# A two-block transformer layer on one core: front sums, last queries and weight pieces dealt anew to the steps of the first attention

## The chip, the cores and the metric

The kernel runs on one NeuronCore of a Trainium2 chip, in one launch. The metric is device time in microseconds. The kernel before takes 1286.5 us, the median of three runs (1285.71, 1286.50, 1286.87).

A core has five engines, each with its own program in order, which meet by semaphores. TensorE (PE) multiplies and transposes into eight PSUM banks, VectorE (DVE) and ScalarE (ACT) do elementwise work, GpSimd (POOL) does elementwise work beside them, and SyncE (SP) issues loads.

## The reference

Two transformer blocks run in turn over 512 tokens of width 1024, in float32. The change touches the first block's attention alone:

```python
h = rmsnorm(x, attn_pre_g); proj = h @ w_in
# sliding window: 8 heads, 2 key heads, window 128, with sinks
o_swa = swa_attention(q_s, k_s, v_s, sinks, slopes[:8])
# 8 more heads, three branches each, every one a softmax of its own
s_c = q . k_cmp   # 31 compressed keys
s_s = q . k_slc   # selected blocks: at 512 tokens, all of them
s_w = q . k_win   # window of 512
o_nsa = g0 * (p_c @ v_cmp) + g1 * (p_s @ v_slc) + g2 * (p_w @ v_win)
mix = concat([o_nsa, o_swa]) @ w_o
x = x + rmsnorm(mix, attn_post_g)
```

Then follow a gated MLP with a depthwise convolution, an embedding gate, and a second block (neighbourhood attention, retention, MLP, final norm).

## The kernel before, in words

**Precision.** Each float32 operand is split into a high and a low part, and a dense product is three matmuls: high weight by high input, high by low, low by high (lines 593, 594 and 595 in `triple`). The input's parts are AH and AL; BH and BL later hold attention's outputs.

**Weights.** A *piece* is 128x512 weights, loaded by SyncE into one of five raw buffers. ScalarE makes its high part (`hi`, L1323), VectorE or, in the attention, GpSimd its low part (`lo`, L2943). TensorE then runs 12 matmuls of 512 columns on it (`part`). Conversion runs four pieces ahead. Pieces go in the order of the list that `plan` builds, and in the attention that order comes from the table `FILL1`: for every step, the pieces that TensorE runs in it.

**Units and steps.** The first attention has 28 units. Units 0 to 7 are sliding-window ("swa"). Then come four rounds of five: one *compressed* unit (units 8, 13, 18, 23) and four wide ones ("sl" and "wn", for two key groups g). A software pipeline runs over steps s:

- TensorE in step s: the pieces of `FILL1[s]`; the transposes of unit s-2 (L813; of a compressed unit L854); the scores of unit s+1 (L799 and L800; compressed L843); the value products of unit s-3 (L826 and L827, the compressed part L866).
- VectorE in step s: the scaling of finished queries or keys (L2095, L2097), the softmax bias and minimum of unit s (L2191; compressed L2233 to L2241), sums of outputs (`out_add` L2214, `out_low` L2219), the low parts of the transposed probabilities of unit s-3 (`rest`, L2207), the reciprocal for unit s-1 (L2272), and last the low parts of new queries (`stacked`, L2109) or keys (`doubled`, L2104 and L2105).
- ScalarE in step s: first what the pieces of step s-1 finished (`filled`: queries L1411, keys L1406 and L1407, or a front sum), the exponentials of unit s (L1510), weights' high parts, the copies of the transposed probabilities of unit s-2 (`turned`, L1516), then `out_part` (L1521), which waits for the values of unit s-3, and `out_high` (L1525).
- GpSimd in step s: the normalising of unit s-1 (L2969), which the transposes of step s+1 need, then low parts of weights.

A piece of "w_swa" or "w_nsa" is half a projection: two make one query pair q(J), J from 0 to 7 (or a key pair). A piece of "w_o_swa" is a whole *front sum*: the sliding-window heads' share of one of the eight blocks of the output projection. ScalarE copies it out of its bank (L1533, `filled`) to ACC1, and the end of attention adds the rest to it.

**Buffers.** The eight banks are handed out in the order in which they are given back, when the program is built. Who takes a bank waits for its last reader. Queries live in four buffers QS, so q(J) waits until the scores that read q(J-2) are done. Low and high keys of the sliding window are in KS1["s"]. The first three ACC1 buffers lie over KS1["s"], the other five over AH, the high input.

## Time and profile before

| | |
|---|---|
| median of the runs | 1286.5 us |
| profiled execution | 1286.42 us, of which the span is 1284.5 us |
| TensorE busy | 1263.0 us, 98% of the span |
| VectorE, ScalarE, GpSimd busy | 786.6, 647.9, 216.9 us |
| chain that ended last | 90% TensorE |
| mean granted clock of TensorE | 0.996 |

The span is the time from the first to the last instruction of the profiled execution. A row of the timeline shows start, duration, engine, line, operands by the program's names and a count; in brackets, the idle time before it and who ended it. Consecutive matmuls overlap at their ends, so what one costs is read from start to start. The whole time is a little over a millisecond; steps 7 to 27 of the first attention run from 100 to 218 us.

### The profile page before, as it was taken

How to read it: one execution, taken by the hardware profiler on the slowest of the kernel's cores; microseconds unless marked ns; L12 is line 12 of the kernel's file. 1: busy time of each engine (PE TensorE's matmuls, PEld its weight loads, DVE VectorE, ACT ScalarE, POOL GpSimd, SP SyncE). 2: the span in 40 equal slices, each digit the busy share in tenths (PEclk: the TensorE clock that was granted, in tenths of full speed). 3: DMA queues.
4: the chain of work that ended last, by engine and by line, in shares of the span. 5: the costliest groups of instructions: out<-in, count | busy, mean ns of one | idle time of the engine just before them, and what ended most of it. 6: DMA issues, size and time to landing. Idle time of an engine off the chain costs nothing.

```text
span 1284.5 us, 16448 instructions
## 1 busy us (share of the span) xinstructions
PE 1263.0 (98%) x6004; PEld 1045.6 (81%) x6004; DVE 786.6 (61%) x1465; ACT 647.9 (50%) x1261; POOL 216.9 (17%) x234
## 2 busy tenths in 40 slices
PE   9999999999999999999999999999999999999998
PEld 8887888878888888888787777887888888888887
DVE  6689687686645565356788876589644343343334
ACT  6787788554335433233555655586533252332344
POOL 0064555000100011001002101032311030110111
PEclk9998999999999999999999999999999999999999
...
GB/s 275 86 50 34 42 41 26 170 82 99 90 100 98 98 90 99 99 96 68 115 91 98 76 56 68 131 112 68 98 99 92 97 75 118 79 115 89 100 90 67
DMA packets 64626, 118.20 MB, mean 92 GB/s; under 512 B 7713, under 2 KB 12193, under 8 KB 64289
## 3 DMA queue, kind: packets, MB, share of 16 engines
...
## 4 chain that ended last, share of the span: by engine, by line
PE 90%; DVE 4%; ACT 2%; issue 2%; DMA 1%; POOL 1%; POOLq 0%; SPq 0%; DVEq 0%; ACTq 0%
PE bank L593 26%; PE bank L595 25%; PE bank L594 25%; PE bank L813 2%; PE bank L693 2%; PE bank L694 2%; PE bank L695 2%; PE bank L826 1%; PE bank L827 1%; PE bank L799 1%; PE bank L800 1%; PE bank L767 1%; DVE q2p L2191 0%; DMA praw<-in_pT 0%; DVE r_bc L2086 0%
## 5 line engine op out<-in xcount | busy, mean ns | idle before, releaser
L2022 DVE TENSOR_TENSOR wl<-raw,wh 128x512 fp32r<-128x512 f32 (+2 forms) x360 | 267.5, 754 | 325.5 <-ACT wh L1323 324.8
L1323 ACT ACTIVATE wh<-raw 128x512 fp32r<-128x512 f32 (+1 forms) x398 | 242.2, 618 | 284.7 <-PE bank L595 273.7
L593 PE MATMUL bank<-AH,wh 128*128 128x512 f32 (+1 forms) x848 | 333.8, 394 | 2.1 <-DVE AL L2036 0.8
L595 PE MATMUL bank<-AH,wl 128*128 128x512 f32 (+1 forms) x848 | 329.3, 388 | 0.0
L594 PE MATMUL bank<-AL,wh 128*128 128x512 f32 (+1 forms) x848 | 327.0, 386 | 0.0
L593 PE MATMUL bank<-BH,wh 128*128 128x512 f32 x624 | 247.7, 397 | 1.6 <-ACT acc L1533 1.6
L595 PE MATMUL bank<-BH,wl 128*128 128x512 f32 x624 | 244.6, 392 | 0.0
L594 PE MATMUL bank<-BL,wh 128*128 128x512 f32 x624 | 243.0, 389 | 0.0
L595 PEld LDWEIGHTS bank<-AH,wl 128*128 128x128 f32 x848 | 159.6, 188 | 35.8
L593 PEld LDWEIGHTS bank<-AH,wh 128*128 128x128 f32 x848 | 159.9, 189 | 35.2 <-issue 2.9
L594 PEld LDWEIGHTS bank<-AL,wh 128*128 128x128 f32 x848 | 159.7, 188 | 33.0 <-issue 0.2
L593 PEld LDWEIGHTS bank<-BH,wh 128*128 128x128 f32 x624 | 117.3, 188 | 27.7 <-ACT acc L1533 2.1
L595 PEld LDWEIGHTS bank<-BH,wl 128*128 128x128 f32 x624 | 117.2, 188 | 27.2
L594 PEld LDWEIGHTS bank<-BL,wh 128*128 128x128 f32 x624 | 117.2, 188 | 25.6 <-issue 0.5
L2985 POOL TENSOR_TENSOR BL<-tmp,BH 128x512 fp32r<-128x512 f32 x22 | 28.6, 1300 | 354.4 <-ACT BH L1632 354.4
L3013 POOL TENSOR_TENSOR AL<-tmp,AH 128x512 fp32r<-128x512 f32 x32 | 40.6, 1303 | 269.6 <-ACT AH L1954 269.6
L2943 POOL TENSOR_TENSOR wl<-raw,wh 128x512 fp32r<-128x512 f32 x38 | 50.2, 1323 | 100.2 <-ACT wh L1323 100.2
L1510 ACT ACTIVATE pp<-pp,small 128x128 f32<-128x128 f32 (+2 forms) x96 | 50.2, 525 | 7.5 <-DVE small L2191 7.1
L2969 POOL TENSOR_SCALAR pp<-pp,small,gates 128x128 f32<-128x128 f32 (+1 forms) x64 | 40.9, 654 | 34.2 <-DVE small L2272 34.2
L2805 DVE TENSOR_TENSOR X<-X,bank 128x512 f32<-128x512 f32 x46 | 31.5, 686 | 24.3 <-PE bank L595 24.2
L2869 DVE SCALAR_TENSOR_TENSOR tmp<-bank,r_bc 128x512 f32<-128x512 f32 x32 | 22.0, 691 | 27.6 <-PE bank L595 16.1
L2191 DVE CUSTOM_DVE_ANT_0 pp<-bank,dn 128x512 f32<-128x512 f32 (+1 forms) x64 | 27.5, 486 | 15.9 <-PE bank L800 15.7
...
## 6 DMA issues: line engine op xcount, KB each, us to landing
raw<-in_w_dn SPq DMA_DIRECT2D x104, 256.0 KB, 2.7
...
```

The costliest lines, as they stand in the source:

```text
L593: t.matmul(o, w, xh, start=start, stop=False, skip_group_check=skip)
L594: t.matmul(o, w, xl, start=False, stop=False, skip_group_check=skip)
L595: return t.matmul(o, wl, xh, start=False, stop=stop, skip_group_check=skip)
L1323: a.activation(W[i % NW].h[:, 0:n], RAW[i % NRAW][:, 0:n], ACT.Copy).then_inc(*s_wh.up(i))
L1510: m = a.activation(o, o, ACT.Exp, bias=m4[:, qb:qb + 1], scale=-1.0, accum_out=s4[:, qb:qb + 1])
L2022: v.tensor_tensor(w.l[:, 0:n], RAW[i % NRAW][:, 0:n], w.h[:, 0:n], ALU.subtract).then_inc(*s_wl.up(i))
L2191: m = v.tensor_tensor_reduce(o, b[:, col:col + w], bias(qb), scale, init, ALU.add, ALU.min, m4[:, qb:qb + 1])
L2805: v.tensor_tensor(chunk(X, c), chunk(X, c), bank.ap(key)[:, :], ALU.add).then_inc(*s_sv.up(done))
L2943: g.tensor_tensor(w.l[:, 0:n], RAW[i % NRAW][:, 0:n], w.h[:, 0:n], ALU.subtract).then_inc(*s_wlg.up(i))
L2969: g.tensor_scalar(o, o, r, by, ALU.mult, ALU.mult).then_inc(*s_nmg.up((u, qb)))
L2985: g.tensor_tensor(x.l, tmp.ap(("u", k))[:, 0:T], x.h, ALU.subtract).then_inc(*s_xlg.up(("ff", k)))
L3013: g.tensor_tensor(x.l, tmp.ap(("rs", 8 * gi + k))[:, 0:T], x.h, ALU.subtract).then_inc(*s_xlg.up(("up", 8 * gi + k)))
```

## The change

- `FILL1` deals the pieces anew. The number of pieces (24) is the same. Steps 13, 14, 18, 19, 23 and 24 now have none; before, it was steps 7, 17, 19, 20, 22, 24 and 25, and step 14 had two. The second half of the "wn" keys, ("w_nsa", 3), moves from step 8 to step 7, the last query piece ("w_nsa", 15) from step 16 to 15, and all eight front sums come after it, from step 16 on.
- The list `QU` names the query buffers: q(0) to q(5) stay in QS, q(6) and q(7) go to KS1["s"], whose readers end with unit 7.
- All eight ACC1 buffers lie over AH; a front sum's copy waits for the last query piece, which is the last reader of AH.
- ScalarE copies a front sum in the step in which TensorE makes it, behind `turned` and before `out_part` (`evicted`).
- The compressed values' split is made by ScalarE in step 7 (before: 8) and by VectorE right behind the softmax of unit 8.

```diff
--- before.py
+++ after.py
@@ -27,10 +27,10 @@
          [(1, 0), (1, 1), (1, 2), (1, 3), (1, 4), (1, 5), (0, 0), (0, 1), (0, 2), (1, 6), (0, 3), (0, 4), (0, 5), (0, 6), (1, 7), (0, 7)]]
 
 FILL1 = {0: [("w_swa", 6), ("w_swa", 7)], 1: [("w_swa", 8)], 2: [("w_nsa", 0), ("w_swa", 9)], 3: [("w_nsa", 1)],
-         4: [("w_nsa", 8)], 5: [("w_nsa", 9)], 6: [("w_nsa", 2)], 8: [("w_nsa", 3)], 9: [("w_nsa", 10)],
...
+         4: [("w_nsa", 8)], 5: [("w_nsa", 9)], 6: [("w_nsa", 2)], 7: [("w_nsa", 3)], 8: [("w_nsa", 10)], 9: [("w_nsa", 11)],
...
 HIDDEN = {("w_swa", 6): 0, ("w_swa", 7): 1}
@@ -298,6 +298,7 @@
         QS = [new(f"qs{i}", T, F32R) for i in range(4)]
         KS1 = {n: [Pair(new(f"ka_{n}{g}", T, F32R), new(f"kb_{n}{g}", T, F32R)) for g in range(2)]
                for n in ("s", "sl", "wn")}
+        QU = QS[0:4] + QS[0:4] + QS[0:4] + [KS1["s"][g].h for g in range(2)] + [KS1["s"][g].l for g in range(2)]
         KCW = [new(f"kc{g}", 64, F32R) for g in range(2)]
         KC1 = [Pair(k[:, 0:32], k[:, 32:64]) for k in KCW]
         V1 = [new(f"v1{b}", 768, F32R) for b in range(4)]
@@ -312,7 +313,7 @@
         dc = new("dc", 124)
         PP.append(new("pp2", 1280))
         OS = [new(f"os{i}", T) for i in range(2)]
-        ACC1 = [at(f"acc1{c}", T, F32, base + 10240 + 2048 * c) for c in range(3)] + [at(f"acc1{c}", T, F32, aA + 2048 * c) for c in range(3, 8)]
+        ACC1 = [at(f"acc1{c}", T, F32, aA + 2048 * c) for c in range(8)]
         cx = at("cx", 1024, F32, aB + 16384)
         cb = [at("cb0", 1024, F32, aB + 20480), at("cb1", 1024, F32, aB)]
         cw1 = [at(f"cw1{i}", 2048, F32, base + 16384 + 8192 * i) for i in range(2)]
@@ -829,14 +830,14 @@
 
             def scores1(u):
                 kind, j, g = unit(u)
-                q, ready = QS[(2 * q_use(u) + g) % 4], s_ql.at(("q", q_use(u), g))
+                q, ready = QU[2 * q_use(u) + g], s_ql.at(("q", q_use(u), g))
                 if kind == "swa":
                     scores(SWA, u, q, KS1["s"][g], ready, s_ql.at(("k", "s", g)), s_qh.at(("k", "s", g, 2)))
                 elif kind == "cmp":
                     b, free = bank.take(("sc", u, 0))
                     e.wait_ge(*free)
                     for g in range(2):
-                        q = QS[(2 * q_use(u) + g) % 4]
+                        q = QU[2 * q_use(u) + g]
                         e.wait_ge(s_ql.at(("q", q_use(u), g)), s_ql.at(("k", "c", g)), s_qh.at(("k", "c", g, 2)))
                         for qb in range(4):
                             c = 64 * (4 * g + qb)
@@ -1443,10 +1444,9 @@
                 t = tmp.ap(("q", J))
                 for g in range(2):
                     if J >= 2:
-                        u = unit_of("swa" if J < 6 else "wn", (J - 2) % 4, g)
-                        L = 1 if u < 8 else 2
-                        e.wait_ge(s_sc.at((u, L)))
-                    stacked(("q", J), g, t, QS[(2 * J + g) % 4], s_sv.at(("q", J)))
+                        u = unit_of("swa", min(J - 2, 3), 1 if J > 5 else g)
+                        e.wait_ge(s_sc.at((u, 1)))
+                    stacked(("q", J), g, t, QU[2 * J + g], s_sv.at(("q", J)))
                 tmp.read(("q", J), (s_ql, ("q", J, 1)))
 
             def pack(kv):
@@ -1524,14 +1524,17 @@
                 e.wait_ge(s_ad.at((*pair, 1)), *free)
                 a.activation(dst.h, src[:, :], ACT.Copy).then_inc(*s_xh.up(pair))
 
+            def evicted(i):
+                key, n = fill_info("w_o_swa", i)
+                e.wait_ge(s_mm.at(("o", key)))
+                e.wait_ge(piece("w_nsa", 15))
+                a.activation(ACC1[i][:, :], bank.ap(key)[:, :], ACT.Copy).then_inc(*s_cp.up(key))
+                bank.read(key, (s_cp, key))
+
             def filled(name, i):
                 key, n = fill_info(name, i)
                 if name == "w_o_swa":
-                    e.wait_ge(s_mm.at(("o", key)))
-                    if i >= 3:
-                        e.wait_ge(piece("w_nsa", 15))
-                    a.activation(ACC1[i][:, :], bank.ap(key)[:, :], ACT.Copy).then_inc(*s_cp.up(key))
-                    bank.read(key, (s_cp, key))
+                    return
                 elif n == 1 and key[0] == "q":
                     queries(key[1])
                 elif n == 1:
@@ -1559,13 +1562,6 @@
                     hidden(1)
                 if s == 2:
                     comp_keys()
-                if s == 8:
-                    e.wait_ge(s_cm.at("vc"), s_z.at("zero"))
-                    for g in range(2):
-                        x = slice(32 * g, 32 * g + 31)
-                        for r in (0, 64):
-                            m = a.activation(VC[g][r + 32 * g:r + 32 * g + 31, half(0)], bank.ap(("vc",))[x, 0:64], ACT.Copy)
-                    m.then_inc(*s_qh.up("vc"))
                 for name, i in later:
                     behind(name, i)
                 if 2 <= s <= N_UNITS + 1:
@@ -1577,6 +1573,16 @@
                     else:
                         v = unit_back(u, 2)
                         turned(SWA if kind == "swa" else NSA, u, PT[buf_of(u)], [s_pv.at(v)] if v >= 0 else [])
+                if s == 7:
+                    e.wait_ge(s_cm.at("vc"), s_z.at("zero"))
+                    for g in range(2):
+                        x = slice(32 * g, 32 * g + 31)
+                        for r in (0, 64):
+                            m = a.activation(VC[g][r + 32 * g:r + 32 * g + 31, half(0)], bank.ap(("vc",))[x, 0:64], ACT.Copy)
+                    m.then_inc(*s_qh.up("vc"))
+                for name, i in FILL1.get(s, ()):
+                    if name == "w_o_swa":
+                        evicted(i)
                 if 3 <= s < N_UNITS + 3 and closes(s - 3):
                     key = out_key(s - 3)
                     n = key[2] + (0 if key[1] == "swa" else 4)
@@ -2143,7 +2149,7 @@
 
             def queries_low(J):
                 for g in range(2):
-                    stacked(("q", J), g, tmp.ap(("q", J)), QS[(2 * J + g) % 4])
+                    stacked(("q", J), g, tmp.ap(("q", J)), QU[2 * J + g])
 
             def pack(kv):
 
@@ -2305,6 +2311,15 @@
                     filled(name, i)
                 if s < N_UNITS:
                     soft1(s)
+                if s == 8:
+                    e.wait_ge(s_qh.at("vc"))
+                    for g in range(2):
+                        x = slice(32 * g, 32 * g + 31)
+                        for r in (0, 64):
+                            m = v.tensor_tensor(VC[g][r + 32 * g:r + 32 * g + 31, half(1)], bank.ap(("vc",))[x, 0:64],
+                                                VC[g][x, half(0)], ALU.subtract)
+                    m.then_inc(*s_ql.up("vc"))
+                    bank.read(("vc",), (s_ql, "vc"))
                 if s >= 4 and closes(s - 4):
                     key = out_key(s - 4)
                     out_add(key, key[3], out_sum(key))
@@ -2320,15 +2335,6 @@
                     g3 = gates[:, :].rearrange("p (b h k) -> p b h k", b=4, h=8)[:, :, :, 0]
                     e.wait_ge(s_fn.at(("gates", 3)))
                     v.tensor_tensor(g3, g3, rowv.unsqueeze(2).broadcast_to([P, 4, 8]), ALU.mult).then_inc(*s_dv.up("gv"))
-                if s == 8:
-                    e.wait_ge(s_qh.at("vc"))
-                    for g in range(2):
-                        x = slice(32 * g, 32 * g + 31)
-                        for r in (0, 64):
-                            m = v.tensor_tensor(VC[g][r + 32 * g:r + 32 * g + 31, half(1)], bank.ap(("vc",))[x, 0:64],
-                                                VC[g][x, half(0)], ALU.subtract)
-                    m.then_inc(*s_ql.up("vc"))
-                    bank.read(("vc",), (s_ql, "vc"))
                 for name, i in later:
                     filled_low(name, i)
                 if s == 2:
```

The order of instructions shows it at three places. First, VectorE behind the softmax of unit 8 (pc), steps 8 and 9. os, BL and ptl are `out_add`, `out_low` and `rest`; kb_wn the keys' low parts; L2191 is printed as ISA. Before:

```order
L2241 TENSOR_TENSOR pc_113<-pc_113,small_66 128x2x4x31 [waits s_sf]
L2214 TENSOR_TENSOR os0_116<-bank0,os0_116 64x512 [waits s_cp]
L2219 TENSOR_TENSOR BL_80<-os1_117,BH_79 128x512 [waits s_xh]
L2207 TENSOR_TENSOR ptl1_110<-bank3,pth1_109 128x512 [waits s_pv,s_th]
L2207 TENSOR_TENSOR ptl1_110<-bank7,pth1_109 128x384 [waits s_th]
L2270 TENSOR_TENSOR small_66<-small_66 128x4 [waits s_ex]
L2272 RECIPROCAL small_66<-small_66 128x4 [waits s_nm]
L2328 TENSOR_TENSOR vc0_104<-bank2,vc0_104 31x64 [waits s_qh]
L2328 TENSOR_TENSOR vc0_104<-bank2,vc0_104 31x64
L2328 TENSOR_TENSOR vc1_105<-bank2,vc1_105 31x64 x2
L2095 TENSOR_TENSOR tmp2_74<-bank4,r_bc_64 128x512 [waits s_ql,s_mm]
```

and now:

```order
L2247 TENSOR_TENSOR pc_113<-pc_113,small_66 128x2x4x31 [waits s_sf]
L2319 TENSOR_TENSOR vc0_104<-bank2,vc0_104 31x64 [waits s_qh]
L2319 TENSOR_TENSOR vc0_104<-bank2,vc0_104 31x64
L2319 TENSOR_TENSOR vc1_105<-bank2,vc1_105 31x64 x2
L2220 TENSOR_TENSOR os0_116<-bank0,os0_116 64x512 [waits s_cp]
L2225 TENSOR_TENSOR BL_80<-os1_117,BH_79 128x512 [waits s_xh]
L2213 TENSOR_TENSOR ptl1_110<-bank3,pth1_109 128x512 [waits s_pv,s_th]
L2213 TENSOR_TENSOR ptl1_110<-bank7,pth1_109 128x384 [waits s_th]
L2276 TENSOR_TENSOR small_66<-small_66 128x4 [waits s_ex]
L2278 RECIPROCAL small_66<-small_66 128x4 [waits s_nm]
L2110 TENSOR_TENSOR kb_wn0_95<-tmp2_74,ka_wn0_94 64x512 [waits s_qh]
L2111 TENSOR_TENSOR kb_wn0_95<-tmp2_74,ka_wn0_94 64x512
```

The compressed values' split (vc) stands ahead of `out_add`, and the low parts of the keys end step 8; before, they stood behind the softmax of unit 9, at the end of step 9. (Line numbers of the changed kernel differ by a few.)

Second, ScalarE around a front sum. pth are the copies of the transposed probabilities, pp the exponentials, os `out_part`, acc the copy of a front sum. Before, steps 18 and 19:

```order
L1516 ACTIVATE pth0_107<-bank0 128x512 [waits s_pv,s_tr]
L1516 ACTIVATE pth0_107<-bank7 128x512 [waits s_tr]
L1516 ACTIVATE pth0_107<-bank6 128x256 [waits s_tr]
L1521 ACTIVATE os1_117<-bank1 64x512 [waits s_xl,s_pv]
L1533 ACTIVATE acc13_121<-bank2 128x512 [waits s_mm]
L1510 ACTIVATE pp1_112,small_66<-pp1_112,small_66 128x512 [waits s_sf]
L1510 ACTIVATE pp1_112,small_66<-pp1_112,small_66 128x384
L1510 ACTIVATE pp1_112,small_66<-pp1_112,small_66 128x128
L1510 ACTIVATE pp1_112,small_66<-pp1_112,small_66 128x256
```

and now, steps 16 and 17:

```order
L1516 ACTIVATE pth0_107<-bank4 128x512 [waits s_tr]
L1516 ACTIVATE pth0_107<-bank2 128x512 [waits s_tr]
L1516 ACTIVATE pth0_107<-bank7 128x256 [waits s_tr]
L1531 ACTIVATE acc10_118<-bank5 128x512 [waits s_mm]
L1525 ACTIVATE BH_79<-os0_116 128x512 [waits s_ad]
L1510 ACTIVATE pp0_111,small_66<-pp0_111,small_66 128x512 [waits s_sf]
L1510 ACTIVATE pp0_111,small_66<-pp0_111,small_66 128x384
L1510 ACTIVATE pp0_111,small_66<-pp0_111,small_66 128x128
L1510 ACTIVATE pp0_111,small_66<-pp0_111,small_66 128x256
L1324 ACTIVATE wh3_60<-raw3_52 128x512 [waits s_raw3]
```

The copy has moved from behind `out_part`, which waits for TensorE (s_pv), to directly behind the copies of the probabilities.

Third, TensorE from the last matmuls of step 16 to the first of step 17. Before:

```order
L799 MATMUL bank6<-ka_wn1_96,qs3_85 128x256 [waits s_sf]
L800 MATMUL bank6<-kb_wn1_97,qs3_85 128x256
L866 MATMUL bank1<-pct_137,vc0_104 128x512 [waits s_tl]
L813 MATMUL bank5<-ident_67,pp1_112 128x128 [waits s_nmg,s_sv]
L813 MATMUL bank5<-ident_67,pp1_112 128x128 [waits s_nmg] x3
L813 MATMUL bank4<-ident_67,pp1_112 128x128 [waits s_sf]
```

and now:

```order
L800 MATMUL bank6<-ka_wn1_96,qs3_85 128x256 [waits s_sf]
L801 MATMUL bank6<-kb_wn1_97,qs3_85 128x256
L867 MATMUL bank0<-pct_137,vc0_104 128x512 [waits s_tl]
L594 MATMUL bank5<-BH_79,wh0_54 128x512 [waits s_wlg,s_cp]
L595 MATMUL bank5<-BL_80,wh0_54 128x512
L596 MATMUL bank5<-BH_79,wl0_55 128x512
L594 MATMUL bank5<-BH_79,wh0_54 128x512
```

Before, step 17 began with transposes; now it begins with a piece whose bank (5) is that of the front sum of step 16, so that it waits for its copy by ScalarE (s_cp).

## Rows read from the trace of the kernel before

**Rows 1.** Waits of TensorE, 95 to 235 us: waiter, releaser, us in total, times, longest
```profile
PE bank L813 <- ACT acc L1533: 2.9, 3, 1.3
PE bank L593 <- ACT acc L1533: 1.6, 2, 1.3
```

**Rows 2.** Busy us of each engine by window, then TensorE's granted clock
```profile
95.00:100.00 5.00, 5.00 (x35) 4.49 (x33) 4.90 (x12) 4.93 (x15) 3.00 (x5) 1.00 0.20 52
...
105.00:110.00 5.00, 5.00 (x17) 4.32 (x17) 4.80 (x9) 3.20 (x10) 2.75 (x4) 0.50 0.29 85
```

**Rows 3.** Timeline of TensorE, 100 to 120 us: start, us, line, operands, count
```profile
100.07 0.33 PE L813 MATMUL bank<-ident,pp 128*128 128x128 f32 x1
...
101.04 1.51 PE L813 MATMUL bank<-ident,pp 128*128 128x128 f32 x6 [0.64 <-POOL pp L2969]
...
103.20 1.86 PE L843 MATMUL bank<-kc,qs 128*128 128x64 f32 x8
...
104.87 0.56 PE L826 MATMUL bank<-pth,v 128*128 128x256 f32 x1
...
106.62 0.73 PE L593 MATMUL bank<-AH,wh 128*128 128x512 f32 x1
...
111.05 0.93 PE L813 MATMUL bank<-ident,pp 128*128 128x128 f32 x7
...
113.97 0.44 PE L593 MATMUL bank<-AH,wh 128*128 128x512 f32 x1
...
116.77 0.93 PE L813 MATMUL bank<-ident,pp 128*128 128x128 f32 x7
...
119.27 0.47 PE L799 MATMUL bank<-ka_wn,qs 128*128 128x512 f32 x1 [1.58 <-issue]
```

**Rows 4.** Timeline of TensorE, 129 to 133 us
```profile
129.71 1.25 PE L813 MATMUL bank<-ident,pp 128*128 128x128 f32 x10
...
130.72 0.48 PE L799 MATMUL bank<-ka_wn,qs 128*128 128x512 f32 x1
...
132.08 0.40 PE L866 MATMUL bank<-pct,vc 128*128 128x512 f32 x1
```

**Rows 5.** Timeline of TensorE, 155 to 185 us
```profile
161.71 0.40 PE L593 MATMUL bank<-AH,wh 128*128 128x512 f32 x1
...
167.08 1.25 PE L813 MATMUL bank<-ident,pp 128*128 128x128 f32 x10
...
178.88 1.31 PE L813 MATMUL bank<-ident,pp 128*128 128x128 f32 x10 [1.31 <-ACT acc L1533]
```

**Rows 6.** Timeline of ScalarE, 155 to 185 us
```profile
165.24 1.32 ACT L1516 ACTIVATE pth<-bank 128x512 fp32r<-128x512 f32 x3
...
166.98 1.27 ACT L1411 ACTIVATE qs<-tmp 64x512 fp32r<-64x512 f32 x2
...
177.61 0.59 ACT L1521 ACTIVATE os<-bank 64x512 f32<-64x512 f32 x1 [1.86 <-PE bank L827]
...
178.22 0.60 ACT L1533 ACTIVATE acc<-bank 128x512 f32<-128x512 f32 x1
```

**Rows 7.** Timeline of VectorE, 110 to 180 us
```profile
110.48 0.88 DVE L2328 TENSOR_TENSOR vc<-bank,vc 31x64 fp32r<-31x64 f32 x4
...
129.38 1.54 DVE L2109 TENSOR_TENSOR qs<-tmp,qs 64x512 fp32r<-64x512 f32 x2
...
171.90 0.48 DVE L2233 TENSOR_TENSOR pc<-bank,dc 128x124 f32<-128x124 f32 x2
...
173.89 1.60 DVE L2207 TENSOR_TENSOR ptl<-bank,pth 128x512 fp32r<-128x512 f32 x3
```

**Rows 8.** Timeline of GpSimd, 125 to 180 us
```profile
129.45 3.30 POOL L2969 TENSOR_SCALAR pp<-pp,small,gates 128x128 f32<-128x128 f32 x4 [0.95 <-DVE small L2272]
...
175.68 2.37 POOL L2969 TENSOR_SCALAR pp<-pp,small,gates 128x128 f32<-128x128 f32 x4 [0.57 <-DVE small L2272]
```

**Rows 9.** VectorE by form, 60 to 232 us: count, busy us, mean ns of one
```profile
L2104 DVE TENSOR_TENSOR kb_wn<-tmp,ka_wn 64x512 fp32r<-64x512 f32 x2 | 1.4, 683 | 0.0
```

6 lines of the change are left out of this document (3 added, 3 removed).

## The prediction

> **What bounds the kernel now.** I read the page first: TensorE is busy for 98% of the span and is 90% of the chain that ended last. So time is won or lost only where TensorE stands still or runs at its lower clock. The work on it is the same before and after: the same pieces, transposes, scores and value products. The question is therefore how much idle or slow time lies where the change reaches, steps 7 to 27 of the first attention, and what new idle time comes.
>
> Next the waits of TensorE there [rows 1]: 2.9 + 1.6 = 4.5 us for a bank that a front sum's copy frees, in five places. The timeline adds 1.58 us once ahead of scores [rows 3]. Then the granted clock by window [rows 2]: 1.00 nearly everywhere, but 0.50 (1.2 instead of 2.4 GHz) from 105 to 110 us. The timeline around it [rows 3] shows what went before: step 7, which has no piece. TensorE did one transpose at 100.07, stood 0.64 us for GpSimd's probabilities, took until 102.94 or so for the other six, and then ran 64-column matmuls; from there it is slow until the piece of step 8 is nearly through.
>
> **What goes away.**
> (a) Steps 7 and 8. Step 7 runs from 100.07 to 106.62, 6.55 us [rows 3]. At full speed it would be: seven transposes, 7/10 of the 1.01 us that ten take [rows 4], 0.7; the small product of the compressed values, 0.3; the compressed scores, at half clock 104.87 - 103.20 = 1.67, so 0.84; the value products, at half clock 106.62 - 104.87 = 1.75, so 0.88. Sum 2.7, so 3.8 us are lost. The piece of step 8 took 111.05 - 106.62 = 4.43 us against 116.77 - 113.97 = 2.80 at full clock: 1.6 more. The change puts a piece of 2.8 us ahead of step 7's transposes. They then begin at about 102.9; GpSimd's last part of these probabilities was there when the six were through, just before 102.6, so there is little left to wait for, and 2.8 us of dense matmuls stand where the thin stretch was. I take all 5.4 us. Bounds: 5.4, and 2.1 if the clock falls all the same.
> (b) The wait of 1.58 us ahead of the scores of unit 10 [rows 3]. "issue" hides its cause; the order shows it: these scores need the "wn" keys' low parts, which VectorE made last in step 9. They are now made in step 8: 1.6 us gained.
> (c) The bank waits, 4.5 us. At 177.61 ScalarE ran `out_part`, for which it had waited for TensorE's value products, and only then the front sum's copy, 178.22 to 178.82; TensorE began its transposes at 178.88, after 1.31 us [rows 5, 6]. Moved ahead of `out_part`, the copy is done before the values are. All five waits go: 4.5.
> Sum of what goes: 11.5 us.
>
> **What comes.** The trace shows no step in the new arrangement, so these are worked out.
> (d) Steps 8 to 10. VectorE was already busy 4.90 of 5.00 us at 95 to 100 [rows 2], where a step of TensorE lasts about 5.4, so a step of VectorE costs 5.3, of which the low parts of a query pair and its scaling are 2.3 (1.54 by [rows 7], and 0.7 for one more pass over 512 columns). Step 8 now holds instead the scaling of the keys, 0.7, their four low parts at 0.68 [rows 9], 2.7, the compressed values' split, 0.9 [rows 7], and a compressed softmax, 171.90 to 173.89, 2.0 against 1.7: in all 7.7. TensorE's step 8 is 2.8 + 0.7 + 1.36 + 0.9 = 5.8 (scores 132.08 - 130.72 = 1.36 [rows 4]). VectorE falls 1.9 us behind, and the low parts of the probabilities, behind these in its queue, are what TensorE's value products wait for in steps 8 to 10. I take 1.9; bounds 0 and 3.5 (all that was moved in: 2.7 and 0.9).
> (e) The pairs of steps without pieces, 13 and 14, 18 and 19, 23 and 24. Before, the second step of such a pair had the cheap transposes of a compressed unit (steps 19 and 20, 24 and 25); now both have a wide unit's. The chain that its transposes need starts with the compressed scores: softmax, `rest` and reciprocal on VectorE, 171.90 to 175.68, then 2.37 us of GpSimd [rows 7, 8], 6.15 in all. TensorE has for this time only values, transposes, scores, values: 1.36 + 1.01 + 1.36 + 1.36 = 5.1. So 1.05 us are missing at each second step, and about 0.3 at its value products, for which `rest` comes late by the same queue. At the first step of a pair a piece lies in between, 2.8 us more, and VectorE has no more to do: 0.1. At steps 13 and 14 the low parts of q(6) stand beside GpSimd's normalising: beside such a stretch (129.38, 1.54 us) it took 3.30 instead of 2.37 [rows 7, 8], 0.9 more, so 1.0 at step 13. Pairs: 2.4 + 1.4 + 1.4 = 5.2. Bounds: 1.5 (VectorE catches up elsewhere) and 8.
> (f) A new bank wait at step 17. Its piece takes the bank of step 16's front sum. In the trace ScalarE was through with the copies of the probabilities of step 16 at 165.24 + 1.32 = 166.56; TensorE's step ran from 161.71 to 167.08 [rows 5, 6]. The queries that stood behind them, 1.27 us [rows 6], now stand ahead (q(7) comes a step sooner), and the front sum's own copy is 0.5 (0.60 less the overlap at its start): done at 166.56 + 1.27 + 0.5 = 168.33, 1.2 after TensorE wants the bank. Steps 22 and 27 have the same form without queries: 167.06, just in time. So 1.2; bounds 0 and 3.6, if the other two come late as well.
> The buffers cost nothing: q(6) and q(7) wait for less than before, and ACC1's wait is for a piece of a step earlier. The moved conversions of weights are four pieces ahead as before, and SyncE's loads with them.
> Sum of what comes: 1.9 + 5.2 + 1.2 = 8.3 us.
>
> Net 11.5 - 8.3 = 3.2 us less than the profiled execution's 1286.42, which lies 0.1 under the median: 1283.2 us for the profile, 1283.3 for the median. What follows the attention is bound by TensorE, so the gain is kept.
>
> In (e), rule and row differ. Beside VectorE's two-input subtractions GpSimd's normalising was 0.93 longer for 1.54 us of them. The Trainium skill (SBUF — State Buffer, section "Who interferes with whom") says that a VectorE instruction with both inputs in SBUF contends with a GpSimd instruction that reads SBUF, and that the one that comes second is blocked for the other's whole duration. By this rule the normalising would be 1.54 longer, and step 13 would cost 0.6 more: the sum would be 2.6 less instead of 3.2. The rule speaks against the change also in step 8, where 2.7 us of such subtractions now meet the normalising of unit 7.
>
> **Rivals.**
> R1, the new waits overlap more than I think. One late VectorE may be what (d) and (e) both count, and a wait at step 13 gives the chain of step 14 its time. Then only about half of 8.3 comes: 7.5 us gained, 1279. For it: what VectorE owes after step 8 is paid once, and each wait of TensorE gives it time. Against: at steps 13 and 14 the chain is a plain sum of durations.
> R2, no change: one wait takes the place of another. If ScalarE is late at steps 17, 22 and 27 (3.6 instead of 1.2) and the pairs cost 6 instead of 5.2, it leaves nothing: 1286.5. The same comes from one fall of the clock, which costs what (a) shows, 0.84 + 0.88 + 1.6 = 3.3 us. For it: ScalarE has 4.93 of 5.00 us of work at 95 to 100 [rows 2].
> R3, slower: the starved pairs lower the clock. At 100 to 103 thin work with two short waits went before the fall [rows 3]; steps 13 and 14 have 2.4 us of waits in some 10 us with no piece. If it falls in two of the three pairs, 6.6 us are lost: 1286.5 - 3.2 + 6.6 = 1289.9. It decides from the second fall on. Against: the wait of 1.31 us ahead of step 19, with no piece until step 21, did not lower it.
> The Trainium skill (TensorE: Matmul & The Clock Gate, section "HAM oscillation — how this bites in real kernels") ties a fall to one long idle gap. The trace does not agree: the longest gap before this fall was 0.64 us, and gaps of 1.3 to 1.6 us lowered nothing. By the page R3 could not come at all.
>
> **Numbers.** Forecast 0.50, R1 0.15, R2 0.25, R3 0.10. A measurement of this kernel tells 0.2% (2.6 us) from no change. The forecast's own range is 1281 to 1285.5, of which about 0.12 lies above 1283.9, so faster is 0.38 + 0.17 = 0.55 with R1 and the best of R2, no change 0.34, slower 0.11. Range for 8 in 10: 1279.5 to 1287.5.
>
> **What would show it.** Right: clock 1.00 from 100 to 115 us; no wait of TensorE of 1.3 us for acc behind `out_part`; about 1.2 us for acc at the piece of step 17; waits of about 1 us for pp at the transposes of steps 13, 14, 19 and 24; small waits for the low parts ptl in steps 8 to 10. Wrong: a window at 0.50 anywhere in steps 13 to 24; waits for acc at steps 22 and 27; or no waits for pp at all, which would be R1.

## The result, and the profile after

The changed kernel takes 1284.07 us, the median of 9 runs (1282.31 to 1285.17), against 1287.16 us for the kernel before in the same runs (1285.71 to 1289.13): ratio 0.9974, 95% interval 0.9966 to 0.9982. It is faster by 0.26%, some 3.3 us. The forecast was 1283.3 us and 3.2 us.

The profiled execution took 1282.31 us with a span of 1280.4 us, and is the fastest of the nine, so its span flatters the change. The page has TensorE busy for 98% of the span and its clock at the highest digit (90% or more) in all 40 slices; the mean granted clock is 0.999. The waits of TensorE from 95 to 235 us (columns as in [rows 1]) are new ones:

```profile
PE bank L814 <- DVE os L2220: 2.7, 2, 1.4
PE bank L814 <- POOL pp L2975: 2.6, 7, 0.4
PE bank L594 <- ACT acc L1531: 1.2, 1, 1.2
```

The 4.5 us in five places of [rows 1] have become 1.2 us in one. Two waits for a bank that VectorE's `out_add` frees stand beside it, and seven small ones for GpSimd's probabilities. By window, with columns as in [rows 2]:

```profile
95.00:100.00 5.00, 5.00 (x35) 4.54 (x34) 4.87 (x11) 4.92 (x15) 3.00 (x4) 1.00 0.18 54
100.00:105.00 5.00, 5.00 (x35) 4.30 (x34) 4.76 (x17) 4.44 (x15) 3.86 (x7) 1.00 0.14 52
105.00:110.00 5.00, 5.00 (x31) 4.30 (x29) 4.86 (x10) 4.84 (x14) 2.10 (x3) 1.00 0.17 56
...
135.00:140.00 5.00, 3.96 (x24) 2.94 (x24) 4.86 (x13) 3.53 (x10) 4.42 (x7) 1.00 0.09 10
140.00:145.00 5.00, 3.60 (x26) 3.23 (x26) 3.90 (x14) 3.69 (x11) 2.98 (x4) 1.00 0.28 93
```

The window from 105 to 110 us has a clock of 1.00, where it was 0.50 [rows 2]. The holes are now at 135 to 145 us, in steps 13 and 14, and the clock stays at 1.00 through them. The places of the waits, in TensorE's timeline (columns as in [rows 3]):

```profile
99.34 0.45 PE L594 MATMUL bank<-AH,wh 128*128 128x512 f32 x1
...
102.15 0.93 PE L814 MATMUL bank<-ident,pp 128*128 128x128 f32 x7
...
107.95 0.93 PE L814 MATMUL bank<-ident,pp 128*128 128x128 f32 x7
...
116.10 0.55 PE L814 MATMUL bank<-ident,pp 128*128 128x128 f32 x3 [1.31 <-DVE os L2220]
...
118.64 0.45 PE L594 MATMUL bank<-AH,wh 128*128 128x512 f32 x1
...
136.05 0.33 PE L814 MATMUL bank<-ident,pp 128*128 128x128 f32 x1 [0.31 <-POOL pp L2975]
...
136.69 0.33 PE L814 MATMUL bank<-ident,pp 128*128 128x128 f32 x1 [0.31 <-POOL pp L2975]
...
137.44 0.99 PE L814 MATMUL bank<-ident,pp 128*128 128x128 f32 x7 [0.42 <-POOL pp L2975]
...
142.65 1.31 PE L814 MATMUL bank<-ident,pp 128*128 128x128 f32 x10 [1.40 <-DVE os L2220]
...
159.05 0.50 PE L594 MATMUL bank<-BH,wh 128*128 128x512 f32 x1 [1.17 <-ACT acc L1531]
...
224.31 0.40 PE L594 MATMUL bank<-BH,wh 128*128 128x512 f32 x1
```

The first row is the piece of step 7. The step's seven transposes now run without a wait (second row; before: 1 and 6, with 0.64 us between [rows 3]). Step 9 waits 1.31 us, step 13 0.31 + 0.31 + 0.42 us, step 14 1.40 us, step 17 1.17 us. The row at 118.64 is the first matmul of step 10's piece; the last row is the first matmul of w_o_nsa, where the reach of the change ends.

**A yardstick.** Two executions of one program can differ in their first 26 us. The matmul over r_bc that ends this part, in the kernel before, in the changed kernel, in the changed kernel run a second time, and in the changed kernel with late copies (below), whose program is the same up to there:

```profile
23.77 1.02 PE L706 MATMUL bank<-r_bc,ones 128*128 128x512 f32 x2
```

```profile
5.59 0.96 PE L681 MATMUL bank<-wh,AH 128*128 128x408 f32 x4 [1.15 <-ACT wh L1324]
...
23.15 1.02 PE L707 MATMUL bank<-r_bc,ones 128*128 128x512 f32 x2
```

```profile
24.79 1.02 PE L707 MATMUL bank<-r_bc,ones 128*128 128x512 f32 x2
```

```profile
5.66 1.70 PE L681 MATMUL bank<-wh,AH 128*128 128x408 f32 x4 [0.85 <-ACT wh L1324]
...
25.69 1.02 PE L707 MATMUL bank<-r_bc,ones 128*128 128x512 f32 x2
```

So I measure each trace from this matmul to the first one of w_o_nsa, and call it **the stretch**. It was 228.35 - 23.77 = 204.58 us before and 224.31 - 23.15 = 201.16 us after: 3.42 us less. The second trace of the changed kernel, whose time is 1.9 us longer (1284.19 against 1282.31 us), gave 201.21 us, a difference of 0.05 us. That is one pair of traces, and three other traces show more: all programs here are alike up to step 7, and the transposes of step 6 start 73.61 to 73.67 us after the matmul over r_bc in eleven traces, but 73.79 us in e11, 73.89 us in e1 and 74.09 us in e8. So a stretch can be off by up to 0.5 us, and where the clock falls a single trace shows only one of the depths that it can fall to (see e7). Behind the stretch nothing changed: 1284.5 - 228.35 = 1056.2 us before, 1280.4 - 224.31 = 1056.1 us after.

### The profile page after: what moved, and what is told of

It is laid out like the page before. It is cut to its first block, busy times and chain, and to the rows that moved or that the text cites. A ratio compares the mean times of both kernels' runs of the same rounds, so it can differ in the third digit from the quotient of the medians.

```text
span 1280.4 us, 16447 instructions
## 1 busy us (share of the span) xinstructions
PE 1260.2 (98%) x6004; PEld 1042.5 (81%) x6004; DVE 785.4 (61%) x1465; ACT 647.5 (51%) x1261; POOL 218.4 (17%) x234
## 4 chain that ended last, share of the span: by engine, by line
PE 88%; DVE 7%; issue 2%; ACT 2%; POOL 1%; DMA 0%; POOLq 0%; DVEq 0%; ACTq 0%
PE bank L594 25%; PE bank L596 25%; PE bank L595 25%; PE bank L814 2%; PE bank L694 2%; PE bank L696 2%; PE bank L695 2%; PE bank L800 1%; PE bank L827 1%; PE bank L801 1%; PE bank L828 1%; POOL pp L2975 1%; DVE q2p L2197 1%; DVE ptl L2213 1%; PE bank L768 1%
## 5 line engine op out<-in xcount | busy, mean ns | idle before, releaser
L2975 POOL TENSOR_SCALAR pp<-pp,small,ones 128x256 f32<-128x256 f32 (+1 forms) x32 | 23.1, 734 | 78.4 <-DVE small L2278 78.4
```

Of the source, the lines that this page charges most:

```text
L2975: g.tensor_scalar(o, o, r, by, ALU.mult, ALU.mult).then_inc(*s_nmg.up((u, qb)))
```

## The experiments

Twelve runs were made, of the changed kernel once more and of eleven other kernels, each timed beside the kernel before: e6 rests on 6 executions, e11 on 5, the others on 9 to 11; "of before" is the ratio to it in the same runs.

| kernel | of before (95%) | stretch, us |
|---|---|---|
| before | 1 | 204.58 |
| changed | 0.9974 (0.9966 to 0.9982) | 201.16 |
| changed, again | 0.9975 (0.9965 to 0.9984) | 201.21 |
| e1 copies alone | 0.9998 (0.9989 to 1.0007) | 204.63 |
| e2 keys early alone | 0.9990 (0.9981 to 0.9999) | 203.37 |
| e3 changed, copies late | 0.9999 (0.9990 to 1.0008) | 203.26 |
| e4 changed, even table | 0.9991 (0.9983 to 1.0000) | 202.10 |
| e5 changed, `out_add` first in step 9 | 0.9976 (0.9966 to 0.9985) | 201.02 |
| e6 changed, copy ahead of `pth` | 0.9969 (0.9957 to 0.9981) | 200.12 |
| e7 changed, step 7 empty | 1.0011 (1.0002 to 1.0020) | 204.01 |
| e8 changed, hybrid table | 0.9972 (0.9963 to 0.9981) | 201.33 |
| e9 e1, weights behind | 0.9989 (0.9978 to 0.9999) | 202.11 |
| e11 changed, a piece in 13 | 0.9969 (0.9956 to 0.9981) | 200.90 |
| e12 changed, low parts later | 0.9998 (0.9989 to 1.0007) | 203.96 |

**The yardstick run.** The changed kernel, unedited.

> The changed kernel once more, unedited, as the yardstick of this group and of the four kernels already timed. It is run because two executions of programs that are alike up to that point can differ in their first 26 us: the matmul over r_bc starts at 23.15 us in the changed kernel's trace and at 25.69 us in that of the kernel with late copies, and all that follows keeps the distance. Theory 1 (an execution has this start or the other, whatever the kernel): median 1283.4 to 1285.2, 0.9966 to 0.9982 of the kernel before as before, single executions spread over about 2.5 us, and from that matmul to the first w_o_nsa matmul 201.2 us +-0.2 in the trace. Rival (the slow start goes with a chip or a group of runs, and all comparisons between groups are off by it): median 1286 or more.

Measured: median 1283.53 us, ratio 0.9975, stretch 201.21 us. Theory 1 holds: same kernel, start at 24.79 instead of 23.15 us, and the same from there on to within 0.06 us.

**e7, term (a) undone.**

```
-7: [("w_nsa", 3)], 8: [("w_nsa", 10)],
+8: [("w_nsa", 3), ("w_nsa", 10)],
```

> The changed kernel with term (a) alone undone: w_nsa 3 goes from step 7 back to step 8, which then holds two pieces, and step 7 holds none, as in the kernel before. Theory (TensorE's clock falls when step 7 has no dense piece, and that is worth 3 to 5 us): the granted clock is 0.50 to 0.85 in one or two of the 5 us windows between 100 and 115 us (counted with the slow start 2.6 us later), the mean clock 0.996 to 0.998, and the median 3 to 5.5 us above the changed kernel's of this group, that is no better than the kernel before. Rival (with two pieces in step 8 the stall of about 1 us in step 7 stays, but the clock doesn't fall or falls for a shorter time): 0.5 to 2 us above. Second rival (step 8's second piece covers what step 7 lost): within 0.5 us.

Its windows, with the clock in the column ahead of the DMA share:

```profile
100.00:105.00 5.00, 3.77 (x25) 2.80 (x24) 4.84 (x17) 4.44 (x14) 3.83 (x6) 0.95 0.12 36
105.00:110.00 5.00, 5.00 (x19) 4.13 (x19) 4.54 (x14) 2.89 (x10) 2.84 (x4) 0.71 0.23 71
```

The clock falls again, and the gain is gone: 1.0011 / 0.9975 = 1.0036, some 4.6 us (about +-1.7, from the two intervals). The profiled execution shows only 2.85 us in its stretch, but it is one of the milder: 1287.23 us at a mean clock of 0.996, where 7 of the 11 executions had 0.995 and took 1289.0 to 1290.7 us. The wait of 1.6 us ahead of step 9's scores is back too, which I had not expected: the "wn" keys' low parts fall again into VectorE's step 9. But the changed kernel's wait of 1.31 us in step 9 is gone with it, and steps 8 and 9 together (from the transposes of step 8 to the piece of step 10) take 10.46 us here and 10.69 us in the changed kernel. So what this run loses, it loses in step 7 and the pieces beside it: it prices (a).

**e2, the keys alone.** The kernel before with w_nsa 3 in step 7, and the conversions of the compressed values where the change puts them.

```
-6: [("w_nsa", 2)], 8: [("w_nsa", 3)], 9: [("w_nsa", 10)],
+6: [("w_nsa", 2)], 7: [("w_nsa", 3)], 9: [("w_nsa", 10)],
```

> The kernel before with the other part alone: the second piece of the wn keys in step 7 instead of step 8, and the compressed values' split a step earlier on ScalarE and earlier on VectorE. All else as before. My account: the clock stays at 2.4 GHz in steps 7 and 8 (5.2 us back) and the wait of 1.6 us ahead of the scores of unit 10 goes; but now step 8 has no piece while VectorE's and GpSimd's part of it is full (the low parts of the keys beside the normalising of unit 7), so that TensorE waits some 3 to 4 us in steps 8 and 9. Net 2 to 4 us less than before, and the five waits for front sums (4.5 us) stay. Rival: the clock fell for another reason than step 7's thin stretch, and falls again: no gain, a window at 0.50 near 105 us.

It gave 1.2 us in the stretch and 0.1% in the median, less than the 2 to 4 us expected. TensorE's timeline and windows say why:

```profile
110.35 0.51 PE L799 MATMUL bank<-ka_sl,qs 128*128 128x512 f32 x1 [1.89 <-DVE vc L2313]
```

```profile
105.00:110.00 5.00, 3.44 (x27) 2.77 (x25) 4.72 (x13) 4.92 (x16) 3.29 (x5) 1.00 0.17 56
110.00:115.00 5.00, 4.51 (x18) 4.01 (x19) 4.86 (x12) 4.11 (x9) 1.94 (x2) 0.64 0.20 54
115.00:120.00 5.00, 5.00 (x20) 4.06 (x19) 4.84 (x15) 2.56 (x9) 3.23 (x4) 0.68 0.11 21
```

The fall has only moved. Step 8 now has no piece, TensorE waits 1.89 us in it for VectorE, and the clock is down to 0.64 and 0.68 there. Of the tables run, only those with a piece in step 7 and another in step 8 kept the clock at 1.00 there.

**e1, the copies alone.** The kernel before, with the copy of a w_o_swa bank in its own step ahead of `out_part`.

```
+                for name, i in FILL1.get(s, ()):
+                    if name == "w_o_swa":
+                        evicted(i)
                 if 3 <= s < N_UNITS + 3 and closes(s - 3):
```

The old place, in `filled`, is empty.

> The kernel before with one part of the change: ScalarE copies a front sum in its own step, behind the copies of the probabilities and ahead of out_part. Table, buffers and the rest as before. My account: the five bank waits (4.5 us) go, but at steps 19 and 24 the probabilities of GpSimd come next, ready only about 0.5 us after TensorE wants them (178.05 against 177.57 in the trace of before). The fall of the clock in steps 7 and 8 and the wait ahead of the scores of unit 10 stay. So 3 to 4 us less than before, ratio 0.9970 to 0.9977. Rival (the wait only changes its name): under 1.3 us less, and TensorE's waits for pp grow to 3 us or more.

A clear miss: no wait for acc is left, and nothing is gained. TensorE's waits from 95 to 235 us:

```profile
PE bank L813 <- POOL pp L2976: 1.6, 4, 0.6
PE bank L799 <- issue: 1.6, 1, 1.6
PE bank L813 <- DVE os L2221: 1.5, 2, 1.0
...
```

At steps 19 and 24 the waits of 1.31 and 1.30 us have another name: 0.21 us for pp with 0.53 us for `out_add`, and 0.97 us for `out_add`. That takes 1.7 of the 4.5 us. For the rest, compare VectorE and GpSimd in step 20, first in e1, then in the kernel before:

```profile
179.18 1.28 DVE L2271 TENSOR_TENSOR small<-small,gates 128x8 f32<-128x8 f32 x1
...
179.13 1.29 POOL L2950 TENSOR_TENSOR wl<-raw,wh 128x512 fp32r<-128x512 f32 x1 [2.93 <-ACT wh L1323]
```

```profile
181.03 0.17 DVE L2264 TENSOR_TENSOR small<-small,gates 128x8 f32<-128x8 f32 x1
...
181.60 1.30 POOL L2943 TENSOR_TENSOR wl<-raw,wh 128x512 fp32r<-128x512 f32 x1 [3.55 <-ACT wh L1323]
```

A multiplication of 128x8 elements took 1.28 instead of 0.17 us and ended 0.04 us after GpSimd's low part of the weights. With the copy elsewhere ScalarE came earlier to the weights' high part, and GpSimd with it. The same stands at 148.07 and 203.90 us.

**e9, the same without the meeting.** e1, with ScalarE's `behind(name, i)` of steps 15, 19 and 24 behind the turned copies.

```
+                if s in (15, 19, 24):
+                    for name, i in later:
+                        behind(name, i)
...
```

> The kernel with the copies alone moved into their step (all else as before the change), and beside that ScalarE's conversion of the next weights behind instead of ahead of the turned copies in steps 15, 19 and 24, so that GpSimd's low part of these weights starts later. In the trace of the kernel with the copies alone, VectorE's multiplication of 128x8 elements, small<-small,gates, takes 1.28 us at 148.07, 179.18 and 203.90, where it takes 0.17 us in the kernel before; each time it ends with GpSimd's wl<-raw,wh (179.13 + 1.29 us). Theory (VectorE's operations with two SBUF inputs and GpSimd's shut each other out, and these meetings ate about 2.2 us of what the moved copies gave): in steps 20 and 25 the operation takes 0.17 us again, the first attention from the matmul over r_bc to the first w_o_nsa matmul takes 202.4 to 203.4 us instead of 204.6, and the median is 1 to 2.2 us below that of the copies alone, 0.9980 to 0.9992 of the kernel before. Rival (the meetings only stood in for waits that come anyway, since VectorE is what these steps wait for): the same operation takes 0.17 us, but the stretch is within 0.4 us of 204.6 and the median within 0.1% of the kernel before.

```profile
180.84 0.17 DVE L2275 TENSOR_TENSOR small<-small,gates 128x8 f32<-128x8 f32 x1
...
182.18 1.28 POOL L2954 TENSOR_TENSOR wl<-raw,wh 128x512 fp32r<-128x512 f32 x1 [4.30 <-ACT wh L1323]
```

In steps 20 and 25 the operation takes 0.17 and 0.18 us again (at 149.75 it still takes 1.28), and the stretch is 202.11 us, 2.5 us under e1's. Of these 2.5 us, 0.3 stand ahead of step 7, where the two programs are alike; the other 2.2 us are twice the 1.11 us that the operation had been longer, the upper end of the 1.2 to 2.2 us expected. The medians, 0.9989 against 0.9998, say 1.2 us, which is not clear of their noise (about +-1.8). So of the 4.5 us of waits about 1.7 were renamed, and of the other 2.8 some 2.2 were eaten by two meetings of VectorE and GpSimd.

**e3, everything but the copies.** The changed kernel, with the copy again at the start of the next step.

```
                 if name == "w_o_swa":
-                    return
+                    evicted(i)
...
-                for name, i in FILL1.get(s, ()):
-                    if name == "w_o_swa":
-                        evicted(i)
```

> The changed kernel with the old place of a front sum's copy: at the start of ScalarE's next step, behind out_part and out_high. The new table stays. My account: in the new table the front sums stand in steps after which a piece or a compressed unit follows, so that hardly any bank is wanted at once; only the pieces of steps 17, 22 and 27 wait 0.3 to 0.6 us longer. So 0.5 to 1.8 us slower than the changed kernel (ratio to before 0.9978 to 0.9988). Rival (the new place of the copy is what the change lives by): 4.5 us slower than the changed kernel, no better than before.

Its waits for acc are 3.4 us in three places (1.7, 0.87 and 0.87 us, at the pieces of steps 17, 22 and 27) against 1.2 in one, and its stretch is 2.1 us longer than the changed kernel's; the medians' ratio, 0.9999 / 0.9974, says 3.2 us (about +-1.5). I had expected 0.5 to 1.8. By the stretches the copy alone was worth 0 us, the rest of the change alone 204.58 - 203.26 = 1.3 us, both 3.4 us. By the medians it is 0.3, 0.1 and 3.3 us, each good to some 1.2 us.

**e5, step 9's wait.** VectorE's `out_add` of unit 5 ahead of the softmax. In the changed kernel's trace, VectorE, ScalarE and GpSimd:

```profile
110.77 0.65 DVE L2110 TENSOR_TENSOR kb_wn<-tmp,ka_wn 64x512 fp32r<-64x512 f32 x1
...
113.58 0.69 DVE L2197 CUSTOM_DVE_ANT_0 pp<-bank,dn 128x512 f32<-128x512 f32 x1
...
115.34 0.69 DVE L2220 TENSOR_TENSOR os<-bank,os 64x512 f32<-64x512 f32 x1
...
111.58 0.59 ACT L1521 ACTIVATE os<-bank 64x512 f32<-64x512 f32 x1
...
110.97 3.92 POOL L2975 TENSOR_SCALAR pp<-pp,small,ones 128x128 f32<-128x128 f32 x4 [3.87 <-DVE small L2278]
```

```
+                if s == 9 and closes(s - 4):
+                    key = out_key(s - 4)
+                    out_add(key, key[3], out_sum(key))
                 if s < N_UNITS:
                     soft1(s)
...
-                if s >= 4 and closes(s - 4):
+                if s >= 4 and s != 9 and closes(s - 4):
```

> The changed kernel with VectorE's out_add of unit 5 ahead of the softmax of step 9 instead of behind it; nothing else moves. In the changed kernel's trace TensorE waits 1.31 us in step 9 for the bank that this out_add frees; the out_add starts at 115.34, behind four low parts of the keys and the softmax, while ScalarE's half of it was done at 112.17. Theory (the VectorE order in steps 8 to 10 is what the 1.9 us of term (d) are made of): the wait goes, the matmuls from step 9 on come 1.0 to 1.3 us earlier and the median is 0.7 to 1.3 us below the changed kernel's of this group. Rival (the softmax, 0.6 us later, is the next thing late: its pp reach the transposes of step 11 later, or GpSimd's norm): the median is within 0.4 us of the changed kernel's, and a new wait of 0.6 to 1.3 us stands in steps 10 to 12.

The wait of 1.31 us is gone, and step 9's transposes end 1.3 us earlier from the matmul over r_bc. But at step 10 it is 0.75 us, at step 11 0.4, at step 13 0.14, and the stretch is 0.15 to 0.2 us shorter. That is the rival. In the changed kernel VectorE is busy for 43.21 of 45 us from 90 to 135 us. My reading is that it sets the pace there, and that TensorE's idle time only changes place.

**e12, step 13's norm.** The two low parts of step 12 behind the compressed softmax of step 13 on VectorE.

```
                     soft1(s)
+                if s == 13:
+                    for name, i in kept:
+                        filled_low(name, i)
...
-                for name, i in later:
-                    filled_low(name, i)
+                if s == 12:
+                    kept = later
+                else:
+                    for name, i in later:
+                        filled_low(name, i)
```

> The changed kernel with VectorE's two low parts of queries of step 12 (ka_s<-tmp,ka_s, 1.55 us, two SBUF inputs) behind the compressed unit's softmax of step 13 instead of ahead of it. In the changed kernel they run beside GpSimd's norm of unit 11, which takes 3.29 us there and 2.37 us elsewhere, and TensorE waits 0.31 + 0.31 + 0.42 us for it in step 13. Theory (they shut each other out for the length of each operation): the norm takes 2.37 to 2.9 us, the three waits sum to 0.1 to 0.7 us, and step 13's transposes end 0.4 to 0.9 us earlier after the matmul over r_bc than 115.3 us. What is left of it at w_o_nsa is 0.2 to 0.9 us if the wait of 1.40 us in step 14 moves with it. Rival (the norm takes 3.3 us whatever VectorE does, from its own operands): no wait changes and the times are the changed kernel's within 0.2 us.

GpSimd's norm and its next low part of weights, VectorE's two low parts, and TensorE's scores of step 13; then TensorE's window with the clock:

```profile
136.22 2.61 POOL L2981 TENSOR_SCALAR pp<-pp,small,gates 128x128 f32<-128x128 f32 x4 [2.27 <-DVE small L2278]
...
138.79 1.70 POOL L2955 TENSOR_TENSOR wl<-raw,wh 128x512 fp32r<-128x512 f32 x1
...
138.30 2.74 DVE L2115 TENSOR_TENSOR ka_s<-tmp,ka_s 64x512 fp32r<-64x512 f32 x2
...
141.82 0.53 PE L800 MATMUL bank<-ka_sl,qs 128*128 128x512 f32 x1 [1.95 <-DVE ptl L2213]
```

```profile
140.00:145.00 5.00, 3.18 (x11) 2.69 (x12) 4.57 (x13) 0.61 (x2) 2.61 (x5) 0.71 0.20 54
```

```profile
141.00:142.00 1.00, 0.18 (x1) 0.18 (x2) 0.97 (x3) 0.00 (x0) 0.00 (x0) 1.00 0.38 35
142.00:143.00 1.00, 1.00 (x4) 0.70 (x5) 0.85 (x4) 0.00 (x0) 0.12 (x1) 0.57 0.61 236
...
146.00:147.00 1.00, 0.20 (x2) 0.00 (x0) 0.14 (x1) 0.77 (x2) 0.49 (x1) 1.00 0.00 0
```

The norm is 2.61 instead of 3.29 us, the waits at step 13 sum to 0.66 instead of 1.04 us, and its transposes end 0.7 us earlier: the low parts were what lengthened the norm. The kernel is 2.8 us slower in the stretch all the same. The low parts now meet GpSimd's weights (2.74 us for two that took 1.55), and `rest` stands behind them on VectorE. Step 13's scores take the bank that `rest` reads, wait 1.95 us for it, and right behind this wait the clock falls: 1.00 up to 142 us, 0.57 in the next, 1.00 again from 146 us on, 0.71 over the five. Step 14's transposes still wait their 1.40 us, when the clock is back. I had not looked at what would stand behind the low parts.

**e6, step 17's wait.**

```
                 for name, i in later:
                     behind(name, i)
+                for name, i in FILL1.get(s, ()):
+                    if name == "w_o_swa":
+                        evicted(i)
...
```

> The changed kernel with the copy of a w_o_swa bank ahead of the turned pth copies of its step on ScalarE instead of behind them. In the changed kernel one such copy is waited for: in step 17 for 1.17 us, where it stands behind 1.32 us of turned copies (158.83 to 160.05). Theory (term (f) is this order): the wait in step 17 goes or falls under 0.4 us, no other wait for a copy comes, and the stretch up to w_o_nsa is 0.6 to 1.2 us under the changed kernel's 201.2 us. Rival (the turned copies, 0.6 us later in nine steps, delay the values' matmuls and the out_part behind them, or VectorE's rest): the wait goes but the stretch is within 0.3 us of 201.2 us or longer.

No wait for acc is left, and the stretch is 200.12 us, 1.04 to 1.09 us less: term (f) is this order, and the 1.17 us were nearly all real. The median, 0.9969 (0.9957 to 0.9981), agrees but can't tell it from the changed kernel's.

**e4, e8 and e11, other tables.** The later pieces in steps 14, 15, 17, 19, 20, 22, 24, 25, 27 (e4), 14, 15, 17, 19, 20, 22, 25, 26, 27 (e8), and 13, 15, 17, 19, 20, 22, 25, 26, 27 (e11); the edit of e11, the others being alike:

```
-12: [("w_nsa", 14)], 15: [("w_nsa", 15)], 16: [("w_o_swa", 0)],
-17: [("w_o_swa", 1)], 20: [("w_o_swa", 2)], 21: [("w_o_swa", 3)], 22: [("w_o_swa", 4)], 25: [("w_o_swa", 5)],
+12: [("w_nsa", 14)], 13: [("w_nsa", 15)], 15: [("w_o_swa", 0)],
+17: [("w_o_swa", 1)], 19: [("w_o_swa", 2)], 20: [("w_o_swa", 3)], 22: [("w_o_swa", 4)], 25: [("w_o_swa", 5)],
```

> The changed kernel with another table from step 13 on: pieces in steps 14, 15, 17, 19, 20, 22, 24, 25 and 27 (the last query piece in 14) instead of 15, 16, 17, 20, 21, 22, 25, 26 and 27. So no two neighbouring steps are without one. My account: the waits of steps 13 to 14, 19 and 24 came from two steps in a row without a piece; a piece ahead of the transposes of steps 14, 19 and 24 hides them, 1.5 + 1.1 + 1.1 us, and the bank wait of 1.2 us at step 17 goes, since step 16 has no front sum. New: 0.4 us at the scores of steps 16, 21 and 26, whose bank is the last values'. Net 3 to 4 us less than the changed kernel, ratio to before 0.994 to 0.9955. Rival (VectorE and ScalarE, not the place of the pieces, set the pace from step 13 on): under 1 us of difference to the changed kernel.

> The changed kernel with other steps for the later pieces: 14, 15, 17, 19, 20, 22, 25, 26, 27 instead of 15, 16, 17, 20, 21, 22, 25, 26, 27. The even table (14, 15, 17, 19, 20, 22, 24, 25, 27) was 1.6 to 2.1 us ahead of the changed kernel at the transposes of steps 16 to 22 (counted with its extra piece) and lost that, and 1 us more, from step 26 on, where it has no piece in step 26; this table keeps the changed kernel's end. Theory (what the even table lost is only in its last steps): 1.0 to 2.0 us below the changed kernel's of this group. Rival (VectorE sets the pace of the last steps whatever TensorE does before them, so that being early there is worth nothing): within 0.5 us, with as much more waiting for pp or for VectorE in steps 23 to 29.

> The changed kernel with the later pieces in steps 13, 15, 17, 19, 20, 22, 25, 26, 27: as the table tried before with 14 as its first, and only that piece one step earlier. With it in 14, step 13 kept its waits for GpSimd's norm (0.28, 0.31 and 0.42 us) and two waits of 0.3 and 0.2 us came in steps 16 and 17. Theory (a piece ahead of step 13's transposes covers the norm, 3.3 us there): these three waits go, worth about 1.0 us at the transposes of step 13; of that 0.3 to 1.0 us is left at w_o_nsa, 200.2 to 200.9 us after the matmul over r_bc. Rival (VectorE, busy 97% from 90 to 135 us, sets the pace, and TensorE is late for it whatever stands ahead): 201.0 to 201.8 us, with waits of the same sum in later steps.

e4 is 0.9 us longer in the stretch, e8 is within 0.2 us, e11 0.3 us shorter (e8 had lost 0.5 us and e11 0.2 us already ahead of step 7, where nothing differs). e4 and e8 gave what their rivals said, e11 the lower end of its theory. e8 is 2.0 us ahead of the changed kernel at step 17, with as many pieces done. Then come 0.57 us for pp at step 18 and, later, 0.32, 0.58 and 0.97 us, and at the end of step 24 it is 0.2 us behind. e11 has no wait left in step 13 and is 1.7 us ahead at its transposes, and 0.3 at the end. These tables all have six steps without a piece among steps 13 to 27, as the changed one has; a wait removed at one comes back at the next. The lowest ratios are those of e6 and e11, both 0.9969, but their intervals take in the changed kernel's 0.9974. The two edits together were not run.

## Why the prediction was right

The size and the sign came out. The two timelines can be cut at the rows shown, and then each of three parts is near its forecast; inside the last two, terms are wrong and make up for each other.

- *Step 7 and the pieces beside it*, term (a). Before, step 7 and the piece behind it took 111.05 - 100.07 = 10.98 us [rows 3]. Now the piece of step 7, the step, and the piece behind it take 107.95 - 99.34 = 8.61 us, with 2.8 us more of piece in them: 5.2 us gained, 5.4 forecast.
- *Steps 8 and 9*, up to the piece of step 10, (b) less (d). 121.50 - 111.05 = 10.45 us before, 118.64 - 107.95 = 10.69 us now: 0.2 us lost, 0.3 forecast.
- *From step 10's piece to w_o_nsa*, (c) less (e) and (f). 228.35 - 121.50 = 106.85 us before, 224.31 - 118.64 = 105.67 us now, with 2.8 us less of piece: 1.6 us lost, 1.9 forecast.

The one row of the kernel before that [rows 3] leaves out is the start of step 10's piece:

```profile
121.50 0.45 PE L593 MATMUL bank<-AH,wh 128*128 128x512 f32 x1
```

The three make the 3.4 us of the stretch, but for 0.1 us that lie ahead of step 7. Now the terms.

(a) 5.4 us for steps 7 and 8. Shown: the clock stays at 1.00, the step has no wait, 5.2 us are gained, and e7, which takes this back, loses 4.6 +-1.7 us. It carries the result: e7, the change without it, is 0.11% slower than the kernel before. The size depends on the execution (see below).

(b) 1.6 us for the "wn" keys, and (d) 1.9 us for a late VectorE in steps 8 to 10. The wait of (b) is gone, and back in e7, where the waits of (d) are gone: one is the price of the other, and together they are worth 0.2 us of loss. For (d) alone, steps 8 and 9 are some 2.0 us longer than their work. Step 8 is 0.5 us longer than before, and there the trace has what was forecast: the value products' weight loads are held 0.4 us for `rest`. The other 1.5 us are in step 9 and not as forecast: the transposes wait 1.31 us for the bank of unit 5, whose `out_add` stands behind four low parts and a softmax. The sum of durations in (d) was short, too. It took the compressed softmax of step 8 at 2.0 us, from a later unit, but one multiplication of it (`pc`) ran beside GpSimd's low part of weights and took 1.58 us, where the compressed units of steps 13 and 18 have 0.65 and 0.43:

```profile
105.79 1.58 DVE L2247 TENSOR_TENSOR pc<-pc,small 128x248 f32<-128x248 f32 x1
...
105.81 1.29 POOL L2949 TENSOR_TENSOR wl<-raw,wh 128x512 fp32r<-128x512 f32 x1
```

The kernel before has the same at 106.50 (1.51 us), and in e7 it takes 0.52 us. What it costs alone wasn't run.

(c) 4.5 us for the copies, taken as a gain of its own. Wrong as that: e1 gives nothing. Of the five waits the sum needed only that they go, and they go; but 1.7 us would have been other waits and 2.2 us were lost to two meetings that no term had. In the changed kernel the copy's place is worth 2.1 us (e3).

(e) 5.2 us for the pairs. The pair 13 and 14 cost about 3.4 us instead of 2.4, the pairs 18 and 19 and 23 and 24 1.1 and 1.3 instead of 1.4 each; the waits for pp named at steps 19 and 24 are only 0.42 us each, where the forecast looked for about 1. At step 13 it is GpSimd's norm, as predicted (3.29 us beside two low parts). At step 14 the norm was ready, and another chain was late: the values end at 141.25, ScalarE's `out_part` starts at 141.29, `out_add` at 141.91, the transposes that need this bank at 142.65. Without a piece between values and transposes, TensorE waits for these two passes, 1.40 us. The prediction didn't name it.

(f) 1.2 us at step 17: 1.17 us, and e6 gives 1.04 of it back. Steps 22 and 27 have no such wait, as predicted.

With these amounts the last part would be 4.5 - 5.8 - 1.2 = 2.5 us of loss, where the timelines have 1.6. So terms overlap by some 0.9 us, R1 in small; which of them isn't shown. That the whole came out within 0.2 us is partly luck. R3, a fall of the clock in the starved pairs, did not come in the traces of the changed kernel, but e12 shows that it was near: there the clock fell behind waits of 0.66 and 1.95 us, in the changed kernel it did not behind 1.04 and 1.40 us.

The rule of the Trainium skill (SBUF — State Buffer, "Who interferes with whom"), that the later instruction is blocked for the other's whole duration, agrees with e1 and e12: 0.17 us became 1.28, up to the end of GpSimd's operation. For the norm beside low parts it asks too much: 0.92 us longer for 1.55 us of them in step 13, and 1.87 us longer (3.92 instead of 2.05) for 2.7 us in step 8. Its other rule (TensorE: Matmul & The Clock Gate, "HAM oscillation — how this bites in real kernels") asks for one long gap. The traces do not agree: in the kernel before and e7 the longest gap ahead of the fall was 0.64 us, and the longest here, the 1.9 us ahead of the falls in e2 and e12, is still shorter than the gap that the page names.
